# Memory-attention queries multiplied from the un-normed sum, the first layer norm applied to the product

## The chip, the cores and the metric

The kernel runs on one core of one Trainium2 chip. The metric is the device time of one execution in microseconds (us). Four engines do the work here: TensorE (PE, with its weight loads shown apart as PEld), VectorE (DVE), ScalarE (ACT) and SyncE (SP), which issues the weight transfers. GpSimd (POOL) issues a handful of transfers early and late. Each engine runs its own instructions strictly in the order in which they are written, and waits on semaphores that the others count up.

## What is computed

Two transformer blocks on 256 tokens of width 1024, in float32. The stretch that is changed lies in the first block, between the hybrid mixer and the attention over a memory of 256 rows:

```python
x = layer_norm(ALPHA * x + h, ln1_g, ln1_b)        # h: output of the mixer, ... @ w_out
h = memory_cross_attention(x, mem, xa_wq, xa_wkv, xa_wo)
x = layer_norm(ALPHA * x + h, ln2_g, ln2_b)

def layer_norm(x, g, b):
    mu = x.mean(-1, keepdims=True)
    var = square(x - mu).mean(-1, keepdims=True)
    return (x - mu) * rsqrt(var + EPS) * g + b

def memory_cross_attention(x, mem, wq, wkv, wo):
    q = (x @ wq).reshape(B, S, 4, 256)             # four heads
    k, v = split(mem @ wkv)
    p = softmax(einsum('bshd,bmhd->bhsm', q, k) * 256 ** -0.5)
    return einsum('bshm,bmhd->bshd', p, v).reshape(B, S, 1024) @ wo
```

## The kernel before

Activations lie transposed: the width on the partitions in 8 tiles of 128, the 256 tokens along a row. `X` holds the residual stream. Every large product is made in three passes of fp32r: an operand is split into a high half (ACT rounds it) and a low half (DVE subtracts), and PE adds high x high, low weight x high, high weight x low (`three`). For activations these halves lie in `INH`/`INL` or in `HIH`/`HIL`, for weights in `hir`/`lor`.

A **unit** is 256 output columns: 8 tiles of the width, two halves of 128 columns, three passes, 48 matmuls. Its weights come as two chunks of 4 tiles (512 KB, in a ring of 6 raw buffers), and each chunk is split on ACT (`hir`, 128x1024) and then on DVE (`lor`, 128x1024) into one of 4 slots. `Ahead.take` writes these splits into the programs of ACT and DVE: before a unit's own work it splits as far as three chunks ahead, where the slot's earlier matmuls stand earlier in the program. The plan also interleaves chunks for a modulation vector of the second block, which only DVE handles (`raw<-raw,cb`, L1628). `ahead.more()` splits one chunk ahead by itself.

The work around the change, in order:

- Four units `("wout", c)` make the mixer's output. After each, DVE adds it to the residual (`resid`, L1614, `X<-X,ps`) and ACT squares the sum (`SQ`, L1253). PE adds up the row sums by one-column matmuls (`row_sums`): an early part over tiles 0 to 5, then tiles 6 and 7. Before the last unit ACT loads the function table for the square root.
- `layer_norm("n1", ...)`: DVE copies the sums (L1888), makes the variance, ACT takes the root (L1267), DVE the reciprocal (L1896). PE spreads mean and reciprocal over the partitions (`spread_bank`, banks `("n1", "mu")` and `("n1", "r")` of PSUM). DVE subtracts and multiplies in `X`, ACT writes the normed high halves into `INH` (L1272) and the affine result into `X` (L1277), DVE the low halves into `INL`.
- Four units `("xq", c)`, one for each head, the first two interleaved tile by tile, read those halves. DVE copies each product to `QC` (`query`, L1936).
- The attention, head by head: `("lx", i)` are the scores of head i, `("px", h)` the transposes, `("ox", h)` the product with the values. DVE takes the maximum (L1949), ACT the exponential (L1297) and the copies. Then four units `("xo", c)` and the second norm.

PSUM has eight banks: three for units (`lin`), five for all else (`att`). Both pools hand out banks in a ring; a bank taken with `hold` is skipped until it is released, and who takes a bank waits until its previous user's reader has signalled.

The kernel already treats two units of the second block, `("q", 2)` and `("k", 2)`, in the way that the change extends: `late_g` multiplies an un-normed input `xg` with a few extra columns behind the 256 tokens (260 in all) and holds the halves of a unit in one bank of `lin` and one of `att`. DVE settles the product there in pieces (L2137, L1614, L1611), and ACT's part of it (L1407) stands after the splits of the next unit.

## Time and profile before

| | us |
|---|---|
| median of 3 runs | 892.78 |
| lowest, highest | 890.99, 893.64 |
| the profiled execution, its own time | 890.62 |
| its span in the trace | 888.8 |
| PE busy | 851.0 |
| DVE busy | 651.0 |
| ACT busy | 483.1 |
| mean granted TensorE clock | 0.977 of full |

The profiled execution spends 1.8 us outside the span. In the trace the four `wout` units end at 184.96 us, the first `xq` matmul starts at 192.11, the first scores at 218.02, and the first `xo` unit at 236.75. In a timeline each row gives start, time from the first start to the last end of what it merges, engine, line, operation, tiles and shapes, how many, and in brackets how long the engine had been idle and for whom. Consecutive instructions overlap a little, so the distance of two starts is what one costs in a queue.

### The profile page before, as it was taken

Reading aid. Unit: us, or ns where it says so; the run is one execution under the profiler, and the core shown is the slowest. Engines: PE = TensorE matmul, PEld = TensorE weight load, DVE = VectorE, ACT = ScalarE, POOL = GpSimd, SP = SyncE. Lnnn points to the kernel's source line nnn. Section 1 sums busy time; section 2 is a strip of 40 time slices with the busy share of each in tenths; the row PEclk is TensorE's granted clock in tenths of the full one; section 3 lists DMA queues with packets and bytes.
Section 4 is the critical chain, followed back from the end, with each engine's and each line's share of the span. In section 5 each row is a group of like instructions: output and inputs, shape, how many; then the busy total and the mean of one; then the engine's idle time right before and its main releaser. Section 6 shows DMA issues by size and latency. Waiting matters only on the chain.

```text
span 888.8 us, 15825 instructions
## 1 busy us (share of the span) xinstructions
PE 851.0 (96%) x6396; PEld 803.5 (90%) x6396; DVE 651.0 (73%) x1011; ACT 483.1 (54%) x708; POOL 7.6 (1%) x17
## 2 busy tenths in 40 slices
PE   8999998999999999999997999999999899999997
PEld 7889986989889999999996999898998899999885
DVE  5787787777668888888867895787897866655553
ACT  5643456555447666655546745465646654444452
POOL 0200000000000000000000000000000000000000
PEclk9999999979999999999998999999998899999999
DMA  9886658737052765567852554475565276775751
GB/s 336 230 274 210 214 172 257 223 113 255 26 164 92 222 188 186 174 202 254 265 200 71 154 179 132 132 240 184 186 204 159 80 255 214 236 232 180 177 193 48
DMA packets 139592, 166.89 MB, mean 188 GB/s; under 512 B 5520, under 2 KB 123280, under 8 KB 139520
## 3 DMA queue, kind: packets, MB, share of 16 engines
q1 hardware_dynamic: 137712, 162.82, 57.8%
q0 software_dynamic: 720, 2.02, 1.2%
q8 instruction: 50, 0.82, 0.4%
q10 hardware_dynamic: 1088, 1.05, 0.3%
q14 instruction: 22, 0.18, 0.1%
HBM read 164.62 MB, written 1.25 MB: 187 GB/s over the span
## 4 chain that ended last, share of the span: by engine, by line
PE 67%; DVE 19%; ACT 7%; issue 4%; DMA 1%; SPq 1%; DVEq 0%; ACTq 0%
PE ps L520 66%; DVE lor L1611 7%; DVE FA L1611 3%; DVE FA L1614 3%; ACT hir L1104 2%; DMA raw<-in_w_in 1%; DVE FA L1617 1%; DVE raw L1628 1%; DVE X L1611 1%; DVE INL L1611 1%; ACT FA L1297 0%; DVE FA L2297 0%; ACT FA L1230 0%; ACT FA L1490 0%; DVE X L1614 0%
## 5 line engine op out<-in xcount | busy, mean ns | idle before, releaser
L1611 DVE TENSOR_TENSOR lor<-raw,hir 128x1024 fp32r<-128x1024 f32 (+1 forms) x267 | 309.7, 1177 | 110.8 <-ACT hir L1104 107.5
L1104 ACT ACTIVATE hir<-raw 128x1024 fp32r<-128x1024 f32 (+1 forms) x257 | 260.5, 1032 | 125.6 <-PE ps L520 112.6
L520 PE MATMUL ps<-INH,hir 128*128 128x256 f32 (+1 forms) x1064 | 306.5, 288 | 5.1 <-ACT INH L1272 2.5
L520 PE MATMUL ps<-INH,lor 128*128 128x256 f32 (+1 forms) x1064 | 302.7, 285 | 3.3 <-DVE lor L1611 3.3
L520 PE MATMUL ps<-INL,hir 128*128 128x256 f32 (+1 forms) x1064 | 303.2, 285 | 1.5 <-DVE INL L1611 1.3
L520 PEld LDWEIGHTS ps<-INH,hir 128*128 128x128 f32 x1064 | 204.6, 192 | 8.2 <-issue 5.8
L520 PEld LDWEIGHTS ps<-INH,lor 128*128 128x128 f32 x1064 | 204.2, 192 | 5.5 <-DVE lor L1611 4.3
L520 PEld LDWEIGHTS ps<-INL,hir 128*128 128x128 f32 x1064 | 203.9, 192 | 3.0 <-DVE INL L1611 2.8
L520 PE MATMUL ps<-HIH,hir 128*128 128x256 f32 x688 | 196.9, 286 | 0.0
L520 PE MATMUL ps<-HIH,lor 128*128 128x256 f32 x688 | 194.1, 282 | 2.3 <-DVE lor L1611 2.3
L520 PE MATMUL ps<-HIL,hir 128*128 128x256 f32 x688 | 193.2, 281 | 0.0
L520 PEld LDWEIGHTS ps<-HIH,hir 128*128 128x128 f32 x688 | 129.8, 189 | 3.9 <-issue 3.5
L520 PEld LDWEIGHTS ps<-HIH,lor 128*128 128x128 f32 x688 | 129.5, 188 | 3.4 <-DVE lor L1611 2.7
L520 PEld LDWEIGHTS ps<-HIL,hir 128*128 128x128 f32 x688 | 130.0, 189 | 0.0
L1614 DVE SCALAR_TENSOR_TENSOR FA<-ps,vec,FA 128x254 f32<-128x254 f32 (+2 forms) x130 | 53.2, 473 | 14.5 <-ACT FA L1114 14.4
L520 PE MATMUL ps<-hir,HIH 128*128 128x512 f32 (+1 forms) x136 | 52.8, 388 | 6.5 <-DVE HIL L1611 6.5
L1628 DVE SCALAR_TENSOR_TENSOR raw<-raw,cb 128x1024 f32<-128x1024 f32 x48 | 58.3, 1219 | 0.8 <-DMA raw<-in_mod_wT 0.8
L520 PE MATMUL ps<-lor,HIH 128*128 128x512 f32 (+1 forms) x136 | 52.3, 385 | 0.0
L520 PE MATMUL ps<-hir,HIL 128*128 128x512 f32 (+1 forms) x136 | 52.3, 384 | 0.0
L1114 ACT ACTIVATE FA<-ps,vec 128x256 f32<-128x256 f32 x58 | 29.3, 556 | 30.0 <-PE ps L520 30.0
L520 PE MATMUL ps<-FA 128*128 128x256 f32 (+6 forms) x212 | 39.2, 365 | 2.5 <-DVE FA L1611 1.7
L1611 DVE TENSOR_TENSOR HIL<-FA,HIH 128x512 fp32r<-128x512 f32 (+2 forms) x32 | 22.0, 689 | 22.5 <-ACT HIH L1109 21.8
(271 smaller groups left out, 771.0 us busy)
## 6 DMA issues: line engine op xcount, KB each, us to landing
raw<-in_w_in SPq DMA_DIRECT2D x64, 512.0 KB, 4.5
raw<-in_mod_wT SPq DMA_DIRECT2D x48, 512.0 KB, 4.7
raw<-in_ffn_w_up SPq DMA_DIRECT2D x44, 512.0 KB, 4.3
raw<-in_w_ffn_in SPq DMA_DIRECT2D x44, 512.0 KB, 4.6
raw<-in_w_ffn_out SPq DMA_DIRECT2D x22, 512.0 KB, 4.6
raw<-in_ffn_w_down SPq DMA_DIRECT2D x20, 512.0 KB, 4.9
raw<-in_xa_wkv SPq DMA_DIRECT2D x16, 512.0 KB, 4.5
raw<-in_xa_wq SPq DMA_DIRECT2D x8, 512.0 KB, 5.1
```

The costliest lines, as they stand in the source:

```text
L520: return e.matmul(o, l, r, start=start, stop=stop, skip_group_check=True)
L1104: e.activation(hi, src, ACT.Copy).then_inc(*w_hi.up(i))
L1114: e.activation(o[:, b, :], p[:, b * T:(b + 1) * T], ACT.Identity, scale=V(wname, (K - 1) * nb + i + b), bias=V(bname, i + b)).then_inc(*ac ...
L1611: return e.tensor_tensor(o, a, b, op)
L1614: return e.scalar_tensor_tensor(out=o, in0=a, scalar=s, in1=b, op0=op0, op1=op1)
L1617: return e.tensor_scalar(o, a, s1, s2, op0, op1) if op1 else e.tensor_scalar(o, a, s1, None, op0)
L1628: e.scalar_tensor_tensor(out=v, in0=v, scalar=1.0, in1=CB[:, :], op0=MUL, op1=MUL, accum_out=MOD[:, key[1]:key[1] + 1]).then_inc(*dve.up(key))
```

## The change

With G the gains and B the offsets of the first norm, m and r the mean and the reciprocal deviation of a token, and y the un-normed sum, the query is W'(G(y - m)r + B) = (W'Gy - (W'G)m)r + W'B. So:

- `xg1` is a new input in `HIH`/`HIL`: the un-normed sum scaled by `ln1_g` (`gained(c)`, two instructions on ACT and two on DVE for each of the four `wout` units), and two extra columns, `ln1_g` and `ln1_b`, whose products are W'G and W'B.
- The first tile's step of `xq` 0 and 1 stands right behind the last `wout` unit, the second one between the early and the late row sums, the third before the two spreads, the other five after them (`late_g`, 258 columns instead of 256).
- The normed high and low halves in `INH`/`INL` fall away. `X` still gets its norm: DVE's `normed(c)` and eight affine instructions on ACT.
- `query` falls away. In its place stands `settle(c)`: on DVE two copies of two columns, two SCALAR_TENSOR_TENSOR (m(W'G) - product), and one multiplication by r, read from the bank `("n1", "r")`; then on ACT two instructions that negate and add W'B. The scores of head i wait for ACT's `QC` now.
- `xq` units take a bank of `lin` and one of `att` each; the four of `att` are held until all four units have been issued.

```diff
+            g = late_g([("xq", 0), ("xq", 1)], xg1, 2)
+            steps_of(g, 1)
+            row_sums("n1", 3, X[:, 6:8, :], g)
+            steps_of(g, 1)
+            spread_bank(("n1", "mu"), SN[:, 0:2])
+            spread_bank(("n1", "r"), SN[:, 6:8])
+            run(g)
...
+            for c in (2, 3):
+                run(late_g([("xq", c)], xg1, 2))
...
-                    w.wait_ge(copied(before), dve.at(("QC", i)), act.at("KV"))
+                    w.wait_ge(copied(before), act.at(("QC", i)), act.at("KV"))
...
+            def gained(c):
+
+                for k in (2 * c, 2 * c + 1):
+                    w.wait_ge(dve.at(("n1", "x", c)), vec_in.at(0), mm.at("xg1 free"))
+                    e.activation(xg1.hi[:, k, 0:T], X[:, k, :], ACT.Copy, scale=V("ln1_g", k)).then_inc(*act.up(("xg1", "hi", k)))
...
+            def settle(c):
+                for j in range(2):
+                    w.wait_ge(dve.at((("xq", c), "normed")))
+                    e.activation(QC[:, 2 * c + j, :], QC[:, 2 * c + j, :], ACT.Identity, scale=-1.0, bias=GB2[c % 2][j][:, 1:2]).then_inc(
+                        *act.up(("QC", c)))
...
+            for k in range(8):
+                w.wait_ge(dve.at(("n1", "normed", k // 2)))
+                e.activation(X[:, k, :], X[:, k, :], ACT.Identity, scale=V("ln1_g", k), bias=V("ln1_b", k)).then_inc(*act.up(("n1", "affine")))
+            ahead.more()
+            settle(0)
+            ahead.more()
+            settle(1)
+            for c in (2, 3):
+                ahead.unit(("xq", c), 8)
+                settle(c)
...
+            def settle(c):
+
+                key, dst = ("xq", c), QC[:, 2 * c:2 * c + 2, :]
+                for j in range(2):
+                    b, vs = bank["unit", key, j], GB2[c % 2][j]
+                    w.wait_ge(mm.at(("unit", key, j)), *([act.at(("QC", c - 2))] if c >= 2 else []))
+                    e.tensor_copy(vs, b[:, T:T + 2]).then_inc(*dve.up())
+                    w.wait_ge(dve.last(), act.at("mean row"), *before)
+                    stt(dst[:, j, :], MB, vs[:, 0:1], b[:, 0:T], MUL, SUB).then_inc(*dve.up(("out", ("unit", key, j))))
+                w.wait_ge(dve.last(), mm.at(("n1", "r")))
+                tt(dst, dst, over(br[:, 0:T], 2), MUL).then_inc(*dve.up((key, "normed"), ("out", ("n1", "r"))))
```

On ACT, from the root of the norm to the first exponential, this stands before:

```order
L1267 ACTIVATE small<-small 128x2
L1272 ACTIVATE INH<-X,vec 128x256 x4
L1277 ACTIVATE X<-X,vec 128x256 x2
L1272 ACTIVATE INH<-X,vec 128x256 x2
L1277 ACTIVATE X<-X,vec 128x256 x2
L1272 ACTIVATE INH<-X,vec 128x256 x2
L1277 ACTIVATE X<-X,vec 128x256 x2
L1104 ACTIVATE hir<-raw 128x1024 x7
L1297 ACT_TABLE_LOAD
```

and this after, where L1326 is the affine part, L1307 the settling and L1119 the high halves of weight chunks:

```order
L1320 ACTIVATE small<-small 128x2
L1322 ACTIVATE st<-ps 128x256
L1119 ACTIVATE hir<-raw 128x1024 x2
L1326 ACTIVATE X<-X,vec 128x256 x8
L1119 ACTIVATE hir<-raw 128x1024
L1307 ACTIVATE FA<-FA,small 128x256 x2
L1119 ACTIVATE hir<-raw 128x1024
L1307 ACTIVATE FA<-FA,small 128x256 x2
L1119 ACTIVATE hir<-raw 128x1024
L1307 ACTIVATE FA<-FA,small 128x256 x2
L1119 ACTIVATE hir<-raw 128x1024 x2
L1307 ACTIVATE FA<-FA,small 128x256 x2
```

The seven splits, which stood in one piece, stand apart now, with the two instructions of a settled unit between them.

On DVE the same place, from the norm's last product to the third settled unit, reads like this after the change (L1654 `lor` are the low halves of chunks; L2014, L1657 and `FA<-FA,ps` are `settle`):

```order
L1654 TENSOR_TENSOR X<-X,ps 128x512
L1654 TENSOR_TENSOR lor<-raw,hir 128x1024
L2014 COPY small<-ps 128x2
L1657 SCALAR_TENSOR_TENSOR FA<-st,small,ps 128x256
L2014 COPY small<-ps 128x2
L1657 SCALAR_TENSOR_TENSOR FA<-st,small,ps 128x256
L1654 TENSOR_TENSOR FA<-FA,ps 128x512
L1654 TENSOR_TENSOR lor<-raw,hir 128x1024
```

Where two copies of a whole unit stood one behind the other, each unit now has five instructions, with the low half of a chunk ahead of each unit's five.

On PE, with the numbers of the banks, the spreads and the first scores stand like this after the change:

```order
L524 MATMUL ps3<-con,small 128x128 x2
L524 MATMUL ps4<-con,small 128x128 x2
...
L524 MATMUL ps4<-FA 128x256 x4
L524 MATMUL ps5<-FA 128x256 x4
L848 MATMUL ps6<-con,FA 128x128 x4
```

Before, the spreads went to `ps6` and `ps7` and the first scores to `ps3`; now the first scores take `ps4`, the bank of the reciprocal, whose last reader is the fourth `settle` on DVE.

## Rows read from the trace of the kernel before

**Rows 1.** The page's first part: busy time, share, instructions.

```profile
span 888.8 us, 15825 instructions
...
PE 851.0 (96%) x6396; PEld 803.5 (90%) x6396; DVE 651.0 (73%) x1011; ACT 483.1 (54%) x708; POOL 7.6 (1%) x17
```

**Rows 2.** Stretches: length, busy PE, PEld, DVE, ACT, POOL, then PEclk, DMA, GB/s.

```profile
185.00:188.40 3.40, 2.85 (x25) 2.68 (x24) 1.36 (x3) 1.58 (x2) 0.00 (x0) 1.00 0.74 249
188.40:192.00 3.60, 2.25 (x8) 1.86 (x8) 2.29 (x9) 0.80 (x2) 0.00 (x0) 0.50 0.18 60
...
198.00:200.00 2.00, 2.00 (x17) 2.00 (x16) 1.97 (x4) 0.82 (x3) 0.00 (x0) 0.84 0.19 60
...
218.00:220.00 2.00, 2.00 (x12) 1.77 (x11) 0.74 (x2) 0.00 (x0) 0.00 (x0) 1.00 1.00 342
...
222.00:224.00 2.00, 1.19 (x8) 1.12 (x9) 1.48 (x5) 0.41 (x2) 0.00 (x0) 1.00 0.01 3
```

**Rows 3.** Timeline of PE, 184.5 to 226 us.

```profile
184.96 0.28 PE L520 MATMUL ps<-con,st 128*128 128x1 f32 x2
...
186.42 1.05 PE L520 MATMUL ps<-con,X 128*128 128x1 f32 x8 [0.51 <-DVE X L1614]
...
193.34 0.41 PE L520 MATMUL ps<-INH,hir 128*128 128x256 f32 x1
193.55 0.41 PE L520 MATMUL ps<-INH,lor 128*128 128x256 f32 x1
...
218.02 3.62 PE L520 MATMUL ps<-FA 128*128 128x256 f32 x16
222.81 0.66 PE L833 MATMUL ps<-con,FA 128*128 128x128 f32 x4 [1.17 <-DVE FA L1617]
```

**Rows 4.** Timeline of DVE, 165 to 205 us.

```profile
170.52 1.23 DVE L1611 TENSOR_TENSOR lor<-raw,hir 128x1024 fp32r<-128x1024 f32 x1 [1.72 <-ACT hir L1104]
...
183.40 2.36 DVE L1611 TENSOR_TENSOR lor<-raw,hir 128x1024 fp32r<-128x1024 f32 x2 [0.57 <-ACT hir L1104]
185.68 0.68 DVE L1614 SCALAR_TENSOR_TENSOR X<-X,ps 128x512 f32<-128x512 f32 x1
188.40 0.16 DVE L1888 COPY small<-ps 128x4 f32<-128x4 f32 x1 [2.04 <-PE ps L520]
...
189.43 0.17 DVE L1896 RECIPROCAL small<-small 128x2 f32<-128x2 f32 x1 [0.27 <-ACT small L1267]
...
194.92 1.40 DVE L1611 TENSOR_TENSOR X<-X,ps 128x512 f32<-128x512 f32 x2
...
202.70 1.22 DVE L1628 SCALAR_TENSOR_TENSOR raw<-raw,cb 128x1024 f32<-128x1024 f32 x1
```

**Rows 5.** Timeline of ACT, 165 to 198 us.

```profile
180.20 0.63 ACT L1253 ACTIVATE SQ<-X 128x512 f32<-128x512 f32 x1 [2.44 <-DVE X L1614]
...
182.26 1.99 ACT L1104 ACTIVATE hir<-raw 128x1024 fp32r<-128x1024 f32 x2
...
195.38 1.09 ACT L1277 ACTIVATE X<-X,vec 128x256 f32<-128x256 f32 x2
196.38 1.08 ACT L1272 ACTIVATE INH<-X,vec 128x256 fp32r<-128x256 f32 x2
```

**Rows 6.** Timeline of DVE at the settled units of the second block.

```profile
491.55 0.15 DVE L2137 COPY small<-ps 128x3 f32<-128x3 f32 x1
...
492.84 0.69 DVE L1611 TENSOR_TENSOR FA<-FA,st 128x512 f32<-128x512 f32 x1
493.45 0.15 DVE L2137 COPY small<-ps 128x3 f32<-128x3 f32 x1
```

**Rows 7.** Timelines of PE and ACT at the 260-column units.

```profile
461.58 0.29 PE L520 MATMUL ps<-INH,hir 128*128 128x260 f32 x1
461.70 0.28 PE L520 MATMUL ps<-INH,lor 128*128 128x260 f32 x1
...
462.28 0.89 ACT L1365 ACTIVATE INH<-X,small 128x256 fp32r<-128x256 f32 x2
```

## What I predict, and from which rows

> **What bounds the kernel now.** I read the page's busy times first: PE is busy for 851.0 of 888.8 us, DVE for 651.0, ACT for 483.1 [rows 1]. So in most of the program PE sets the pace, and the question is what happens in the one place where it does not. The table by stretches shows that place. Around the first norm PE has only one-column matmuls, the spreads and waits: 2.85 us busy of 3.40 and 2.25 of 3.60, and in the second of these stretches the granted clock is 0.50 (1.2 of 2.4 GHz), after PE had done nothing but one-column matmuls and waited since 184.96. It stays there while the first query matmuls run and is back only within 198 to 200 (mean 0.84 there) [rows 2, 3]. PE's timeline gives the prices: query matmuls start 0.21 us apart at the low clock [rows 3], and the 260-column ones elsewhere 0.12 apart at the full one [rows 7]. The last `wout` matmul is followed at 184.96 by the first row sum, and the first scores start at 218.02 [rows 3]. These 33.1 us hold 192 query matmuls, which at 0.12 are 22.9 us. That is the most that the change could work on: about 10 us, of which some 2.9 are the low clock (30 matmuls at 0.095 more each) and the rest the norm.
>
> Then I read DVE and ACT, because the change gives PE a start without the norm, but gives DVE and ACT more to do, and puts the two in a row.
>
> **The change, part by part.**
>
> *Ahead of the query units.* `gained` adds two ACT instructions per `wout` unit; the nearest row, a scaled copy of 256 columns, is 0.89 for two, about 0.8 in a queue [rows 7]. DVE gets two 256-column instructions, again about 0.8. Before the second unit's splits DVE was idle for 1.72 us for ACT's high half [rows 4]: ACT's extra work (0.8 and 0.3 for the extra columns) lengthens this very wait. So the sums come later by about 1.0 to 1.2 us at unit 2; bounds are 0 (all in idle time) and 1.9 (both units in full). I take 1.2. At unit 3 ACT's chain is square at 180.20, table, high halves at 182.26 [rows 5], low halves at 183.40, residual sum at 185.68 [rows 4]; 0.8 for `gained` goes in between. The last residual sum moves from 185.68 to 185.68 + 1.2 + 0.8 = 187.7.
>
> *PE up to the sums.* The first chunk of `xq` 1 is the first of the two low halves that started at 183.40; it is done at 183.4 + 2.0 + 1.15 = 186.5. PE starts at 184.96 with 6 products, waits until 186.6, does 6 more (187.3), the early sums (0.9: 188.2), the second tile's 12 products (1.4: 189.65) and the late sums, which took 188.40 - 186.42 = 1.98 from their start to DVE's copy [rows 3, 4]: 191.6. DVE's five small instructions take 189.43 - 188.40 = 1.03 to the reciprocal [rows 4]: it is past at 192.75. PE hides its part of this behind products, which is what the change does well; PE is not late for anything from here on.
>
> *DVE's queue behind the reciprocal.* In the order after the change stand three low halves (1.14 each, from 2.36 for two [rows 4]), two modulation chunks (1.14 in a queue [rows 4]) and four pairs that norm `X` (1.40 for two dependent ones, 1.32 in a queue [rows 4]): 3.42 + 2.28 + 5.28 = 10.98, so the last pair is done at 203.75. Before, PE read the normed halves; now nobody does, but this work still stands ahead of the first `settle`.
>
> *ACT in the same place.* Its affine instructions wait for these pairs. The last two (1.09 for two, 1.0 in a queue [rows 5]) end at 204.8, then the high half of the next chunk (0.96 in a queue, 1.05 alone, from 1.99 for two [rows 5]) at 205.85, DVE's low half (0.1 of waiting and 1.14) at 207.1. There `settle(0)` starts. Its inputs have lain in PSUM since about 201.
>
> *The round trip.* This is the term that decides. `settle` on DVE is 1.90 from its first copy to the next instruction, and its last instruction is done 0.08 later: 1.98 [rows 6]. ACT's `settle` waits for that (0.03) and takes 1.0 [rows 5]. The next high half stands behind it on ACT (1.05), the next low half waits for that (0.1 and 1.14), and the next DVE `settle` stands behind the low half. Neither engine has other work in between, apart from one modulation chunk of 1.14 that fits into DVE's wait. One round is 1.98 + 0.03 + 1.0 + 1.05 + 0.1 + 1.14 = 5.3. So the units settle from 207.1, 212.4, 217.7 and, with a second low half in the last round, 217.7 + 5.3 + 1.14 = 224.1. A product unit needs 48 x 0.12 = 5.8, so PE keeps up: it ends its last unit 24 products after the chunk split at 212.4, at about 215.3.
>
> *Who waits for it.* The first scores take the bank that holds r, and so wait for the fourth `settle`: 224.1 + 1.98 + 0.05 = 226.15. Against 218.02 that is **+8.1**. Even with another bank DVE's maximum of the first scores would stand behind the fourth `settle`, so the bank alone costs only some 2. ACT's last two `settle` instructions and its table load run beside the scores. Before, the copy of a unit ran beside PE and this place cost nothing; cover is gone because both engines wait for each other. Bounds: 6 if `gained` hides in idle time and the rounds are 5.0, 9.5 if the sums come 1.9 later and a split waits for its slot on top.
>
> *The clock at the scores.* PE is empty from 215.3 to 226.15. No row shows PE empty for so long here; the nearest are the stretches around the norm, where far less brought 0.50 [rows 2]. So the attention starts at the low clock. Its first two heads' scores take 3.62 at full clock, and the first transposes start 4.8 after the first score [rows 3]; at half they take 7.2, and the transposes follow them: +2.4. If the clock is back half way through, it is +1.7. At the norm it was back some 6 us after the query matmuls began in earnest, so I take **+2.2**; the bounds are 0 (no fall) and the third rival. The later scores and transposes hide behind DVE and ACT as now: PE is busy for 1.19 of 2.00 there [rows 2].
>
> Here the Trainium skill says something else ("TensorE: Matmul & The Clock Gate", "Part 4: PE-mode transpose"): transposes do not count as activity for the clock gate. In both stretches of the attention that stand here, the second of them with transposes, the clock is 1.00 [rows 2], but it came in at full clock. By the rule the attention could stay low for longer after such a start; with the row the term is 2.2, with the rule up to 14.
>
> *At no cost:* the two extra columns (192 x 0.001 = 0.2 us of PE, which has 10.8 to spare); the transfers, which now wait for later splits but have raw buffers loaded ahead; the second norm's wait for `X`, which is done at 204.8.
>
> Sum: 890.62 + 8.1 + 2.2 = 900.9 against the profiled execution's own time. The median of the runs shown lies 2.2 above that execution, which gives 903.1. I take the middle, **902.0**.
>
> **Rivals.**
>
> 1. *PE sets the end (faster).* If the waits between ACT and DVE were shorter than PE's work, the stage would end with PE: 184.96 + 0.9 (first wait) + 22.9 + 2.9 (sums) + 0.8 (spreads) = 212.5, and the scores after the last `settle` at 214.5: -3.5, or 889.3 on the median. It decides from the point where a round costs less than about 2.8, which needs ACT's splits to run ahead of its `settle`; the order of the program speaks against it. For it speaks that PE stays dense and may keep its clock. The Trainium skill's rule points this way ("TensorE: Matmul & The Clock Gate", "Loop structure matters more than you think"): matmuls that stand back to back stay warm, and vector work behind them does not break it. Chance 0.04.
> 2. *The round trip is hidden.* If only DVE's own work counted, 1.14 + 1.90 a unit: last `settle` from 207.1 + 3 x 3.04 + 1.14 = 217.4, scores at 219.4, +1.4, with part of the clock's loss 894 to 896. Chance 0.05, of which 0.02 within the noise.
> 3. *The whole attention at the low clock.* 64 records of the scores' kind at 0.226 and 16 transposes at 0.12 are 16.4 us; at half 32.8 against the 18.7 that the attention takes: +14. With 8.1 that is 915. Against it: at half clock PE would be busy without a pause, and at the norm such a stretch brought the clock back. Chance 0.04.
>
> **How the numbers follow.** The forecast has 0.87. Its own range runs from +6 with a small loss of clock to +9.5 with 3.4: 897.5 to 907. That leaves out the rivals and little else, so it is the range for 8 in 10. A measurement can tell 0.3% (2.7 us) from no change. Faster by more: 0.04. Within: 0.03. Slower by more: 0.93.
>
> **What would show it.** Right: in the profile after, `lor` on DVE waits for ACT's `hir`, and `FA<-FA,small` on ACT for DVE, about 2 to 3 us each, four times; the four settled units start 5.3 apart; the first scores start near 226 and wait for DVE `FA`; PE is empty for about 10 us before; the granted clock there is 0.50. Wrong: rounds under 4 us, or first scores before 220; or PE late for a split, with the idle time spread over its 192 matmuls. The first unknown is the size of the wait at the sums, the second the clock.

## The result, and the profile after

| | before | after |
|---|---|---|
| median of the runs, us | 892.88 | 902.70 |
| lowest to highest | 890.99 to 893.64 | 898.90 to 904.97 |
| ratio, with its 95% interval | | 1.0112 [1.0088, 1.0136] |
| own time of the profiled execution | 890.62 | 902.05 |
| its span | 888.8 | 900.2 |
| mean granted TensorE clock | 0.977 | 0.972 |

The kernel became slower, by 9.8 us. A second measurement of the same two kernels gave 1.0120 [1.0098, 1.0142]. The page's first part barely moved against [rows 1]: each engine has a few microseconds more work, and the span is 11.4 longer, so the time is a wait.

```profile
span 900.2 us, 15860 instructions
...
PE 852.9 (95%) x6396; PEld 804.9 (89%) x6396; DVE 655.2 (73%) x1028; ACT 487.0 (54%) x721; POOL 7.6 (1%) x17
```

One thing has to be set aside before the traces are compared. The first residual sum of the `wout` units starts at 168.12 in before and at 170.86 in after, though the code ahead of it is the same. In thirteen traces of kernels that are all alike up to there it starts anywhere from 167.69 to 171.25. So I take this instruction as the zero of the place, and write distances from it as "+": the first scores of before, at 218.02, stand at +49.90. The end of the place is DVE's copy of the second norm's sums, at +94.95 in before and +104.20 in after: the changed stretch is **9.25 us longer**. Behind it both kernels take the same time to the end of the span within 0.6 us (625.73 and 625.14); over the thirteen traces this rest is 624.25 to 626.97, so whole times can differ by over 2 us with nothing changed in the place.

The end mark has a weakness of its own. Between the fourth residual sum of the `xo` units and the copy lie sixteen one-column matmuls, and the clock falls in them or behind them, at no fixed place. In after, where it stays at 1.00 until 275.5, the copy comes 2.72 behind that residual sum; in e3_fill, the same code there, the clock is at 0.50 from 272.5 and it comes 3.76 behind. The second eight of the sixteen, in after and in e3_fill:

```profile
273.99 1.03 PE L524 MATMUL ps<-con,SQ 128*128 128x1 f32 x8
...
272.77 1.84 PE L524 MATMUL ps<-con,SQ 128*128 128x1 f32 x8
```

So I also give the fourth `xo` residual sum, at +92.23 in before and +101.48 in after: 9.25 by this mark too. Where the two marks differ between runs, the residual sum is free of that part of the clock.

DVE's timeline answers to [rows 4] (start, time, instruction, shapes, count, idle time before and for whom; L1657 `X<-X,ps` are residual sums, L1989 the copy of the norm's sums, L2014 the first instruction of a `settle`, L2035 the first maximum):

```profile
170.86 0.69 DVE L1657 SCALAR_TENSOR_TENSOR X<-X,ps 128x512 f32<-128x512 f32 x1 [0.36 <-PE ps L524]
...
190.33 0.68 DVE L1657 SCALAR_TENSOR_TENSOR X<-X,ps 128x512 f32<-128x512 f32 x1
...
194.37 0.16 DVE L1989 COPY small<-ps 128x4 f32<-128x4 f32 x1 [1.38 <-PE ps L524]
...
205.94 0.69 DVE L1654 TENSOR_TENSOR X<-X,ps 128x512 f32<-128x512 f32 x1
...
208.83 1.23 DVE L1654 TENSOR_TENSOR lor<-raw,hir 128x1024 fp32r<-128x1024 f32 x1 [2.21 <-ACT hir L1119]
209.97 0.15 DVE L2014 COPY small<-ps 128x2 f32<-128x2 f32 x1
...
215.12 0.15 DVE L2014 COPY small<-ps 128x2 f32<-128x2 f32 x1
...
220.26 0.15 DVE L2014 COPY small<-ps 128x2 f32<-128x2 f32 x1
...
224.22 2.36 DVE L1654 TENSOR_TENSOR lor<-raw,hir 128x1024 fp32r<-128x1024 f32 x2 [1.99 <-ACT hir L1119]
226.50 0.15 DVE L2014 COPY small<-ps 128x2 f32<-128x2 f32 x1
...
231.96 0.69 DVE L2035 TENSOR_REDUCE small<-ps 128x2 f32<-128x512 f32 x1 [3.48 <-PE ps L524]
```

The four `settle`s start 5.15, 5.14 and 6.24 apart. ACT's timeline shows the other half of the same wait: each time ACT stands 3.3 us for DVE's product, settles, and only then begins the high half for which DVE waits:

```profile
211.99 0.91 ACT L1307 ACTIVATE FA<-FA,small 128x256 f32<-128x256 f32 x2 [3.29 <-DVE FA L1654]
212.80 1.04 ACT L1119 ACTIVATE hir<-raw 128x1024 fp32r<-128x1024 f32 x1
217.13 0.91 ACT L1307 ACTIVATE FA<-FA,small 128x256 f32<-128x256 f32 x2 [3.28 <-DVE FA L1654]
```

The waits of 155 to 250 us, summed by who waits for whom (us in total, times, longest). The first group was not there before:

```profile
ACT FA L1307 <- DVE FA L1654: 13.3, 4, 3.4
...
PE ps L524 <- DVE FA L1654: 10.1, 1, 10.1
DVE lor L1654 <- ACT hir L1119: 8.9, 7, 2.4
```

The third was 6.7 in 7 before. No wait for a weight transfer is among them; before there were two, of 2.0 and 0.9.

PE's timeline, answering to [rows 3]: the first scores, and the first transposes behind them.

```profile
228.53 5.11 PE L524 MATMUL ps<-FA 128*128 128x256 f32 x16 [10.06 <-DVE FA L1654]
234.81 0.66 PE L848 MATMUL ps<-con,FA 128*128 128x128 f32 x4 [1.16 <-DVE FA L1660]
```

The table by stretches answers to [rows 2] (columns as there). At the norm and in the products the clock stays at 1.00, where before it was 0.50; it falls in PE's empty time and is back within 230 to 232:

```profile
188.40:192.00 3.60, 2.79 (x24) 2.66 (x23) 2.61 (x3) 1.46 (x4) 0.00 (x0) 1.00 0.36 107
192.00:200.00 8.00, 8.00 (x71) 8.00 (x70) 6.04 (x13) 4.41 (x8) 0.00 (x0) 1.00 0.53 160
...
220.00:224.00 4.00, 0.00 (x0) 0.00 (x0) 2.13 (x6) 1.73 (x3) 0.00 (x0) 0.64 0.66 221
224.00:228.00 4.00, 0.00 (x0) 0.00 (x0) 3.67 (x7) 1.07 (x2) 0.00 (x0) 0.50 0.35 115
228.00:230.00 2.00, 1.47 (x4) 1.20 (x5) 0.48 (x1) 1.47 (x3) 0.00 (x0) 0.50 0.81 241
230.00:232.00 2.00, 2.00 (x8) 1.65 (x7) 0.04 (x1) 0.72 (x1) 0.00 (x0) 0.65 0.15 54
```

So what the change is good at, it did: PE ends its query products at +47.6, where before they ended with the first scores at +49.9. Then it stands empty for 10.06 us, because the two engines behind it wait for each other.

### The profile page after: what moved, and what is told of

Same layout as the page of the kernel before. It is cut to its first block, busy times and chain, and to the rows that moved or that the text cites. A ratio compares the mean times of both kernels' runs of the same rounds, so it can differ in the third digit from the quotient of the medians.

```text
span 900.2 us, 15860 instructions
## 1 busy us (share of the span) xinstructions
PE 852.9 (95%) x6396; PEld 804.9 (89%) x6396; DVE 655.2 (73%) x1028; ACT 487.0 (54%) x721; POOL 7.6 (1%) x17
## 4 chain that ended last, share of the span: by engine, by line
PE 65%; DVE 20%; ACT 8%; issue 4%; DMA 1%; SPq 1%; DVEq 0%; ACTq 0%
PE ps L524 65%; DVE lor L1654 7%; DVE FA L1657 3%; DVE FA L1654 3%; ACT hir L1119 2%; DMA raw<-in_w_in 1%; DVE raw L1671 1%; DVE FA L1660 1%; DVE X L1654 1%; ACT FA L1340 0%; DVE FA L2383 0%; PE ps L766 0%; ACT FA L1245 0%; ACT FA L1533 0%; ACT L1134 0%
## 5 line engine op out<-in xcount | busy, mean ns | idle before, releaser
L1654 DVE TENSOR_TENSOR lor<-raw,hir 128x1024 fp32r<-128x1024 f32 (+1 forms) x267 | 309.7, 1177 | 117.5 <-ACT hir L1119 112.6
L1119 ACT ACTIVATE hir<-raw 128x1024 fp32r<-128x1024 f32 (+1 forms) x257 | 260.2, 1031 | 118.8 <-PE ps L524 110.6
L524 PE MATMUL ps<-INH,hir 128*128 128x256 f32 (+1 forms) x1000 | 287.1, 287 | 2.9 <-ACT INH L1602 1.2
L524 PE MATMUL ps<-INH,lor 128*128 128x256 f32 (+1 forms) x1000 | 283.6, 284 | 2.9 <-DVE lor L1654 2.8
L524 PE MATMUL ps<-INL,hir 128*128 128x256 f32 (+1 forms) x1000 | 284.2, 284 | 1.0 <-DVE INL L1654 0.9
L524 PE MATMUL ps<-HIH,hir 128*128 128x256 f32 (+1 forms) x752 | 216.1, 287 | 3.2 <-DVE lor L1654 1.4
L524 PE MATMUL ps<-HIH,lor 128*128 128x256 f32 (+1 forms) x752 | 212.8, 283 | 2.3 <-DVE lor L1654 2.3
L524 PE MATMUL ps<-HIL,hir 128*128 128x256 f32 (+1 forms) x752 | 211.9, 282 | 0.0
L524 PEld LDWEIGHTS ps<-INH,hir 128*128 128x128 f32 x1000 | 191.5, 191 | 5.7 <-issue 4.3
L524 PEld LDWEIGHTS ps<-INH,lor 128*128 128x128 f32 x1000 | 191.0, 191 | 5.1 <-DVE lor L1654 3.9
L524 PEld LDWEIGHTS ps<-INL,hir 128*128 128x128 f32 x1000 | 190.8, 191 | 2.1 <-DVE INL L1654 2.1
L1657 DVE SCALAR_TENSOR_TENSOR FA<-ps,vec,FA 128x254 f32<-128x254 f32 (+2 forms) x130 | 53.2, 473 | 15.1 <-ACT FA L1129 15.1
L524 PEld LDWEIGHTS ps<-FA 128*128 128x128 f32 (+2 forms) x212 | 29.5, 179 | 20.0 <-DVE FA L1654 12.1
```

Of the source, the lines that this page charges most:

```text
L524: return e.matmul(o, l, r, start=start, stop=stop, skip_group_check=True)
L1119: e.activation(hi, src, ACT.Copy).then_inc(*w_hi.up(i))
L1654: return e.tensor_tensor(o, a, b, op)
L1657: return e.scalar_tensor_tensor(out=o, in0=a, scalar=s, in1=b, op0=op0, op1=op1)
```

## The experiments

Theory: the round trip between ACT and DVE in the settled units sets the time, with a small loss from the clock behind it. Rivals: DVE's own work (the normed `X` ahead of the units), the bank of r, and the clock. This table gathers the runs. The stretch is measured as above. The kernel before was timed beside each group (medians 891.46 for e1 to e4, 891.93 for e5 to e8, 890.90 for e9 to e11), so medians of different groups are compared by their ratios. e10_after is the changed kernel once more.

| kernel | median, us | ratio to before [95%] | first scores | first transposes | fourth `xo` sum | stretch | against before |
|---|---|---|---|---|---|---|---|
| before | 892.88 | 1 | +49.90 | +54.69 | +92.23 | 94.95 | |
| after | 902.70 | 1.0112 [1.0088, 1.0136] | +57.67 | +63.95 | +101.48 | 104.20 | +9.25 |
| e1_order | 897.58 | 1.0074 [1.0055, 1.0093] | +52.53 | +59.20 | +96.75 | 100.25 | +5.30 |
| e2_twice | 904.03 | 1.0153 [1.0123, 1.0183] | +60.38 | +67.06 | +104.61 | 107.33 | +12.38 |
| e3_fill | 901.80 | 1.0125 [1.0106, 1.0144] | +57.71 | +62.59 | +100.12 | 103.88 | +8.93 |
| e4_later | 891.08 | 0.9996 [0.9984, 1.0007] | +44.57 | +52.42 | +92.26 | 94.98 | +0.03 |
| e5_bank | 902.01 | 1.0122 [1.0106, 1.0138] | +47.52 | +61.85 | +100.76 | 104.22 | +9.27 |
| e6_norms | 897.26 | 1.0065 [1.0052, 1.0079] | +44.56 | +57.56 | +96.90 | 100.48 | +5.53 |
| e7_best | 886.80 | 0.9950 [0.9938, 0.9963] | +44.56 | +49.34 | +88.72 | 93.06 | -1.89 |
| e8_warm | 891.90 | 1.0006 [0.9990, 1.0022] | +49.73 | +54.51 | +92.05 | 94.77 | -0.18 |
| e9_best | 887.85 | 0.9959 [0.9944, 0.9973] | +44.58 | +49.37 | +87.52 | 90.23 | -4.72 |
| e10_after | 902.94 | 1.0120 [1.0098, 1.0142] | +57.71 | +64.22 | +101.76 | 104.48 | +9.53 |
| e11_fill | 900.56 | 1.0101 [1.0081, 1.0120] | +57.71 | +62.60 | +100.16 | 102.91 | +7.96 |

### The round trip

**e1_order** takes the round trip apart by ACT's order alone; each instruction is still there.

```diff
             ahead.more()
-            settle(0)
             ahead.more()
-            settle(1)
+            settle(0)
             for c in (2, 3):
                 ahead.unit(("xq", c), 8)
-                settle(c)
+                settle(c - 1)
+            settle(3)
```

> The changed kernel with one thing altered: on ScalarE the high halves of the next chunks stand ahead of settle(0), settle(1), settle(2) and settle(3) instead of between them; VectorE's and TensorE's programs are untouched. Theory (round trip): in the changed kernel's trace the settled units start 5.15, 5.14 and 6.24 us apart, because VectorE's low half waits for a high half that waits for ScalarE's settle. Without it the distances fall to VectorE's own work: 3.0 (1.14 + 1.90), 4.2 (a modulation chunk more) and 4.2 (two low halves), in all 11.4 instead of 16.5, so the first scores start 5 us earlier than in the changed kernel and the kernel takes about 897.5. Rival (TensorE or the transfers set the stage): the distances stay, 902.7. Second rival (only the clock costs): distances fall, but the time stays within 1 us of 902.7.

Measured 897.58. That is 5.1 below the changed kernel, but the two were not timed side by side; by the ratios 3.4 of the 10.0 us are back. In the trace of e1_order DVE's settled units follow each other after 3.03, 4.17 and 4.17 us, which is DVE's own work (one low half and one `settle`, in two cases a second half or a modulation chunk):

```profile
206.91 0.15 DVE L2014 COPY small<-ps 128x2 f32<-128x2 f32 x1
...
209.94 0.15 DVE L2014 COPY small<-ps 128x2 f32<-128x2 f32 x1
...
214.11 0.15 DVE L2014 COPY small<-ps 128x2 f32<-128x2 f32 x1
...
218.28 0.15 DVE L2014 COPY small<-ps 128x2 f32<-128x2 f32 x1
```

Its fourth `settle` stands at +50.50 instead of +55.64, the first scores come 5.14 earlier, and the fourth `xo` residual sum 4.73 of the 9.25. Only ACT's order was changed, so about half of the loss is the round trip.

**e2_twice** lengthens it: two more instructions of 256 columns on ACT in each `settle`, that copy `QC` onto itself.

```diff
+                for j in range(2):
+                    w.wait_ge(act.last())
+                    e.activation(QC[:, 2 * c + j, :], QC[:, 2 * c + j, :], ACT.Copy).then_inc(*act.up(("QC", c)))
```

> The changed kernel with two more 256-column instructions on ScalarE behind each settle (a copy of QC onto itself), nothing else. Two such instructions take 0.8 us in a queue, and the second pair waits for the first (some 0.1). Theory (round trip): each of the three rounds grows by 0.9, the first scores start 2.7 us later against the changed kernel (the fourth pair runs beside the scores, and the table load behind it still ends before the first maximum), 905.5 in all. Rival (ScalarE has idle time there, 3.3 us before each settle, so more work on it is hidden): no change, 902.7.

In the trace of e2_twice a round costs 6.04, 6.04 and 7.13 us:

```profile
207.36 0.15 DVE L2017 COPY small<-ps 128x2 f32<-128x2 f32 x1
...
213.40 0.15 DVE L2017 COPY small<-ps 128x2 f32<-128x2 f32 x1
...
219.44 0.15 DVE L2017 COPY small<-ps 128x2 f32<-128x2 f32 x1
...
226.57 0.15 DVE L2017 COPY small<-ps 128x2 f32<-128x2 f32 x1
```

That is 0.9 a round more, on an engine that is busy for half of the time, and the scores come 2.71 later, as expected. If ACT had slack there, it would have cost nothing. Both traces speak for the round trip; the stretch moved by 3.13 here, the median by only 1.3 (904.03, where I expected 905.5), with intervals that overlap, so the times alone do not show it.

### The bank and the normed residual

**e5_bank** frees the bank of r: ACT copies the spread row to SBUF, DVE reads it there.

```diff
+            w.wait_ge(mm.at(("n1", "r")))
+            e.activation(RB, bank["n1", "r"][:, 0:T], ACT.Copy).then_inc(*act.up("r row", ("out", ("n1", "r"))))
...
-                w.wait_ge(dve.last(), mm.at(("n1", "r")))
-                tt(dst, dst, over(br[:, 0:T], 2), MUL).then_inc(*dve.up((key, "normed"), ("out", ("n1", "r"))))
+                w.wait_ge(dve.last(), act.at("r row"))
+                tt(dst, dst, over(RB, 2), MUL).then_inc(*dve.up((key, "normed")))
```

> The changed kernel with one edit: ACT copies the spread reciprocal from its PSUM bank to SBUF, DVE reads it there, and the bank is free for the first scores. This is the step of my prediction that gave the bank alone only some 2 us: with it free the scores run while the last units are settled, but DVE's first maximum still stands behind the fourth settle on DVE, and ACT's table load behind the fourth settle on ACT. From the trace after: the fourth settle ends on DVE at 228.4, ACT's part at 229.4, table load 1.28, first exponentials 1.0, so the first transposes at about 232.7 instead of 234.81: 2.1 us less, part of it given back since the transposes now are the first work after PE's idle time. Theory (round trip sets the time, bank adds about 2): 900.5 to 901.5 where the changed kernel is 902.7. Rival (the wait for the bank, not the round trip, is what the change lost): the whole 8 us come back, 894.

Neither PE's wait nor its size was the loss. The scores run at +47.52, ten microseconds earlier, and the kernel is no faster (902.01, where I expected 900.5 to 901.5). The first transposes did come 2.1 earlier, as expected (+61.85), but now they are the first work after PE's empty time. The stretches of e5_bank show PE empty, the clock fallen, and back only in 231 to 233:

```profile
224.00:229.00 5.00, 0.00 (x0) 0.00 (x0) 2.36 (x8) 3.21 (x7) 0.00 (x0) 0.50 0.59 191
229.00:231.00 2.00, 1.40 (x6) 1.31 (x7) 1.32 (x4) 0.61 (x3) 0.00 (x0) 0.50 0.00 0
231.00:233.00 2.00, 2.00 (x7) 1.61 (x6) 0.78 (x3) 0.89 (x3) 0.00 (x0) 0.58 0.00 0
```

In after, the first scores run while the clock comes back; here the transposes and the second scores do. From the first transposes to the first `xo` residual sum it is 21.37 instead of 19.99. So of the 2.10 some 0.72 are left at the fourth `xo` residual sum, and these are gone in the one-column matmuls behind it, where the clock had fallen (+9.27).

**e6_norms** is e5_bank with the norm of `X`'s tiles 2 to 7 moved from ahead of the first `settle` into the attention.

```diff
             run(late)
-            for c in (1, 2, 3):
-                normed(c)
             ahead.more()
...
                     ts(nmx, mxx, -0.0625, None, MUL).then_inc(*dve.up(("nmx", i)))
+                    if i:
+                        normed(i)
```

> e5_bank and one edit more: the norm of X's tiles 2 to 7 (three pairs on DVE, six affine instructions on ACT) is moved from ahead of the first settle to inside the attention, behind the first maxima and copies. It tells what the normed residual costs where it stands, by itself, with the round trips left as they are. From the trace after: three pairs are 3.96 us in DVE's queue and six affine instructions 3.0 on ACT ahead of the split that settle(0) waits for. Theory: the first settle comes about 4.0 earlier, the rounds stay at 5.15, 5.15 and 6.2, and the attention pays about 1 for the pairs (1.32 each in waits of 1.09): 3 us under e5_bank, about 898. Rival (DVE's own queue is not the bound there, ACT's wait for slots that PE frees is): settle(0) moves by less than 2, and the time by nothing.

The first `settle` stands at 203.82, which is +34.87 instead of +39.11: 4.2 earlier. The rounds stay 5.14, 5.15 and 6.25. The stretch is 3.74 shorter than in e5_bank (3.86 at the fourth `xo` residual sum), the median 4.7 lower, timed side by side. So the work that nobody waits for any more (PE reads other halves now) was the second part of the loss, about 4 us, by standing where it stood.

**e4_later** has all three edits: e1_order's order on ACT, e5_bank's row, e6_norms's place for the norm. Parts of its edit on ACT:

```diff
             ahead.more()
-            settle(0)
             ahead.more()
-            settle(1)
+            settle(0)
             for c in (2, 3):
                 ahead.unit(("xq", c), 8)
-                settle(c)
+                settle(c - 1)
+            settle(3)
...
                     e.activation(PY[:, h % 2, :, :], wide2(bank["px", h]), ACT.Copy).then_inc(*act.up(("out", ("px", h))))
+                    affine(h)
```

> As e1_order, and three things more: ScalarE copies the reciprocal's row to SBUF, so that the bank of the spread is free at once; VectorE's norm of X for tiles 2 to 7 (3.96 us) stands in the attention, behind the maximum of heads 1 to 3, instead of ahead of settle(0); ScalarE's affine part follows it there. Theory (VectorE's queue ahead of the first settle is on the path): the first settle starts 3.8 us earlier than in e1_order, and the first scores about 9 us earlier than in the changed kernel; the norms add at most 0.3 us per head to the attention. 892.5 to 894.5. Rival (TensorE ends the stage, or the norms are paid back in the attention one for one): the same as e1_order, about 897.5.

It is as fast as the kernel before, 891.08 (0.9996 [0.9984, 1.0007]), 1.4 below the range that I expected. At the fourth `xo` residual sum the three parts add up: 4.73 for ACT's order, 0.72 for the bank and 3.86 for the norm make 9.31, and e4_later is 9.22 below after. (By the stretch the two large parts are only 3.95 and 3.74, since in e1_order and e6_norms, and not in e4_later, the clock fell within the one-column matmuls.) What was left shows in the timelines of e4_later, PE's first:

```profile
213.84 3.62 PE L524 MATMUL ps<-FA 128*128 128x256 f32 x16
221.69 1.12 PE L848 MATMUL ps<-con,FA 128*128 128x128 f32 x4 [4.23 <-DVE FA L1666]
```

ACT's, with the fourth settled unit and the load of the function table:

```profile
217.55 0.91 ACT L1307 ACTIVATE FA<-FA,small 128x256 f32<-128x256 f32 x2 [3.26 <-DVE FA L1660]
218.47 1.28 ACT L1345 ACT_TABLE_LOAD   x1
```

DVE's, with two low halves and the start of the fourth `settle`:

```profile
213.26 2.35 DVE L1660 TENSOR_TENSOR lor<-raw,hir 128x1024 fp32r<-128x1024 f32 x2
215.53 0.15 DVE L2020 COPY small<-ps 128x2 f32<-128x2 f32 x1
```

PE is done with the products 5.3 us before the kernel before was, and then waits 4.23 us: two low halves of the next unit stand ahead of the fourth `settle`, and the table of the exponential stands behind it.

### The clock

**e3_fill** keeps PE at work with 70 products into an unused bank, between the last unit and the scores.

```diff
+            j = lin.i % 3
+            w.wait_ge(*[dve.at(("out", ("unit", ("xq", 1), x))) for x in range(2)])
+            for _ in range(70):
+                mul(lin.aps[j][:, 0:256], xg1.hi[:, 0, 0:128], xg1.hi[:, 1, 0:256])
```

> The changed kernel with 70 fp32r matmuls of 256 columns behind the last query unit on TensorE, into a bank that the next unit overwrites; they need 8.3 us of the 10.3 for which TensorE is empty, so the first scores can't come later by them. Theory of the clock term: with TensorE kept busy the granted clock stays at its upper level (1.00 instead of 0.50 to 0.65 in the stretches at 228 to 232), the first two heads' scores take 3.6 instead of 4.7 to 5, and the attention's first maximum comes 1.6 us after the first scores instead of 3.4: 1.6 to 2.4 us off, about 900.8. Rival: the clock has nothing to do with the empty stretch, no change.

The trace of e3_fill, PE's timeline: scores of 3.72 for 16 instead of 5.11, transposes 4.88 behind them instead of 6.28.

```profile
228.48 3.72 PE L524 MATMUL ps<-FA 128*128 128x256 f32 x16 [1.78 <-DVE FA L1658]
233.36 0.66 PE L852 MATMUL ps<-con,FA 128*128 128x128 f32 x4 [1.16 <-DVE FA L1664]
```

The time did not settle it: 1.0125 against 1.0112, where I expected 0.2% less. Both kernels were then timed side by side:

> The changed kernel once more, unedited, on the same chip as e11_fill, since the two had been timed at different occasions, where the kernel before differed by 1.4 us. By the ratio of the first measurement (1.0112) it is 1.1% above the kernel before beside it, 901.5 if that is 891.5. It also shows whether the stage from the first wout residual to the last xo residual is 101.5 again.

> e3_fill once more, unedited, beside e10_after: the changed kernel with 70 product matmuls into an unused bank ahead of the first scores, so that PE comes to them at the full clock. In the traces the stage was 1.36 us shorter than in the changed kernel (100.12 instead of 101.48); the times, taken at two occasions, did not show it. Theory (the low clock costs the change about 1.4): 1.0 to 1.8 us below e10_after. Rival (it costs nothing, what comes late at the scores is waited for elsewhere anyway): equal to e10_after within 0.5.

902.94 and 900.56, 2.4 apart, but the intervals of the ratios overlap ([1.0098, 1.0142] and [1.0081, 1.0120]). The traces agree: the first transposes come 1.36 and 1.62 earlier with the filler, and so does the fourth `xo` residual sum (1.36 and 1.60). I take the clock's price as about 1.5 us; the times are compatible with it and alone don't show it.

The traces also tell why it is no more. The transposes wait for a chain of DVE and ACT that starts with DVE's first maximum, and the maximum needs only the first head's eight scores, not all sixteen. The first maximum in before, and the first maximum and the first transposes in e1_order:

```profile
219.95 0.69 DVE L1949 TENSOR_REDUCE small<-ps 128x2 f32<-128x512 f32 x1 [1.04 <-PE ps L520]
...
224.12 0.69 DVE L2035 TENSOR_REDUCE small<-ps 128x2 f32<-128x512 f32 x1 [3.88 <-PE ps L524]
...
226.98 0.66 PE L848 MATMUL ps<-con,FA 128*128 128x128 f32 x4 [0.52 <-DVE FA L1660]
```

The maximum comes 1.93 behind the first scores in before, 3.43 in after, 3.66 in e10_after, 3.81 in e1_order and 3.83 in e2_twice. The transposes follow it by 2.85 or 2.86 in all five and in both runs with the filler, and the first `xo` residual sum follows them by 20.0 in all seven. In e1_order the clock came back only some 5 us after the scores began, and the lag was still 1.9 above before's.

**e8_warm** looks at the clock on the other side: it puts products between the small matmuls at the norm of the kernel before (`fill(n)` is n products of 256 columns).

```diff
-            layer_norm("n1")
+            row_sums("n1", 3, X[:, 6:8, :])
...
+            fill(3)
+            spread_bank(("n1", "mu"), SN[:, 0:2])
+            fill(4)
+            spread_bank(("n1", "r"), SN[:, 6:8])
+            fill(7)
```

> The kernel before with 14 product matmuls of 256 columns into an unused bank: 3 behind the row sums, 4 behind the spread of the mean, 7 behind the spread of the reciprocal. Nothing else is changed, and their result is not used. It takes the price of the clock out of the 10 us that the change could work on. Theory (some 2.9 us of them are the 30 query matmuls at 0.21 instead of 0.12): the granted clock stays 1.00 from 188.4 on, query matmuls start 0.12 apart, and the kernel is 2 to 2.9 us faster than the kernel before, 888.6 to 889.5 where that is 891.5. Rival (the first query units wait for ACT and DVE anyway, so that the clock costs nothing): no difference; PE then waits for halves between its query matmuls.

No difference (891.90, 1.0006 [0.9990, 1.0022]). But the edit did not do all that it was meant to: the clock still fell, to 0.50 in 190 to 192. It came back earlier, in the stretch 192 to 194 instead of 198 to 200. Then PE waits for what the low clock had hidden, as its timeline shows (the first row is the first query matmul):

```profile
193.87 0.36 PE L520 MATMUL ps<-INH,hir 128*128 128x256 f32 x1
...
194.71 0.39 PE L520 MATMUL ps<-INL,hir 128*128 128x256 f32 x1 [0.37 <-DVE INL L1623]
...
196.81 0.39 PE L520 MATMUL ps<-INL,hir 128*128 128x256 f32 x1 [0.42 <-DVE INL L1623]
...
199.08 0.39 PE L520 MATMUL ps<-INL,hir 128*128 128x256 f32 x1 [0.58 <-DVE INL L1623]
```

With the clock up, the first products are paced by DVE's normed low halves, 2.1 and 2.3 us apart; with the clock down, in before, a tile's twelve products at 0.21 take 2.6 and PE does not wait. The fillers themselves made the first query matmul 0.61 later (+24.60 instead of +23.99), and from it to the first scores it is 25.13 instead of 25.91. So the clock there was worth 0.8 of the 2.9 us that I had put down to it, as far as this run shows it, and the fillers took that back. What a clock that never falls would give stays open.

### A version that is faster than both

**e7_best** is e4_later with what its trace asked for. Parts of the edit, against e4_later; `preload` stands on ACT, all else on DVE:

```diff
             for c in (2, 3):
+                ahead.limit = AHEAD if c == 2 else 0
                 ahead.unit(("xq", c), 8)
                 settle(c)
...
+            preload(ACT.Exp)
             settle(3)
...
-                    if i:
-                        normed(i)
+                    if i < 2 and ahead.room():
+                        ahead.stage()
...
+                    if h < 2:
+                        normed(h + 1)
...
+                if c == 0:
+                    normed(3)
```

> From the version with the splits ahead of the settling and the norms of X later (891.1, its trace: fourth settle at 215.53, reduce 217.43, first transposes 221.69 at the low clock, 7.9 us behind the first scores). Edits: on DVE the two low halves of the first output unit are moved from ahead of the fourth settle into the first two waits for the exponentials; ACT loads the table of the exponential ahead of its fourth settle; the pairs of X's norm go into waits of 0.77 and behind the first output unit's splits. Theory: the fourth settle starts as soon as PE is done, at about 214.1, the reduce follows at 216.0, the transposes at about 218.9, 5.1 us behind the scores as in the kernel before, so PE is idle for 1.4 us only and keeps its clock; the first residual sum of the output units comes 4.5 to 5 us earlier: 886 to 887, faster than both kernels. Rival (something else, such as the transfers of weights or DVE's low halves in the attention, sets the time once this is gone): over 889.

886.80, ratio 0.9950 [0.9938, 0.9963]: faster than the kernel before by 0.5%. The fourth `settle` starts 0.34 after PE, and the attention begins as dense as before the change, at the full clock, 5.35 us earlier than there (+49.34 against +54.69). DVE's timeline of e7_best:

```profile
212.09 0.16 DVE L2026 COPY small<-ps 128x2 f32<-128x2 f32 x1 [0.34 <-PE ps L525]
...
214.18 0.69 DVE L2047 TENSOR_REDUCE small<-ps 128x2 f32<-128x512 f32 x1
```

PE's timeline of e7_best:

```profile
212.25 3.62 PE L525 MATMUL ps<-FA 128*128 128x256 f32 x16
217.03 0.66 PE L849 MATMUL ps<-con,FA 128*128 128x128 f32 x4 [1.16 <-DVE FA L1672]
```

**e9_best** cuts the moved norms in two and puts each half into a gap of its own on DVE.

```diff
                     if i < 2 and ahead.room():
                         ahead.stage()
+                    if i >= 2:
+                        (norm_sub, norm_mul)[i - 2](1)
...
-                    if h < 2:
-                        normed(h + 1)
+                    (norm_sub, norm_mul)[h % 2](2 + h // 2)
...
-                if c == 0:
-                    normed(3)
```

> e7_best with the norm of X put into shorter gaps. In e7_best the first residual sum of the output units waited 1.24 us for ACT's last affine instructions (it started at 240.68, the second at 245.36, 4.7 behind instead of 5.7), and the pairs of 1.32 stood in waits of 0.77. Edits: each norm is cut into its subtraction and its multiplication, 0.61 each, one for each wait of DVE in the attention (two for the exponentials of heads 2 and 3, four behind the copies of the product with the values), and the affine instructions follow in the same heads, the last ahead of the splits. Theory: the residual sum no longer waits, the attention loses the 0.5 per head that the pairs cost, and the stage from the first wout residual to the last xo residual shrinks from 88.7 to about 87: 885 to 886. Rival (PE in the output units is bound by other things, and the late sum cost nothing): within 0.5 us of e7_best, 886.8.

The residual sum no longer waits. The fourth `xo` residual sum comes 1.20 earlier than in e7_best. The stretch shrank by 2.83, to 90.23, but the other 1.63 lie in the one-column matmuls behind that sum, where the clock was at 0.50 in e7_best and at 1.00 in e9_best. The median is 887.85, where I expected 885 to 886: level with e7_best, since the intervals [0.9944, 0.9973] and [0.9938, 0.9963] overlap. A gain of 1.2 is less than these times can show.

## Why the prediction came out right

The forecast was 902.0 with 897.5 to 907.0; the measured median is 902.7. Step by step, each as the distance from the first residual sum (168.12 in before, from whose times the forecast counts, 170.86 in after):

| step of the prediction | forecast | measured |
|---|---|---|
| last residual sum (187.7) | +19.58 | +19.47 |
| sums reach DVE (191.6) | +23.48 | +23.51 |
| last pair of the norm done (203.75) | +35.63 | +35.77 |
| first `settle` (207.1) | +38.98 | +39.11 |
| second, third (212.4, 217.7) | +44.28, +49.58 | +44.26, +49.40 |
| fourth `settle` (224.1) | +55.98 | +55.64 |
| first scores (226.15) | +58.03 | +57.67 |
| first transposes (222.81 + 8.1 + 2.2) | +64.99 | +63.95 |

- *Ahead of the units.* The size was right (1.9 for 2.0), and so was the wait: the low half at 170.52 for which DVE was idle for 1.72 [rows 4] starts at +3.40 instead of +2.40, and the next residual sum, the second unit's, stands at +6.83 instead of +5.83.
- *DVE's queue and the round trip.* Right, 5.15 for 5.3. The price of a `settle` on ACT was 0.81 in its queue, not 1.0: I had taken it from affine instructions with two vectors [rows 5], while `settle` has a constant scale. e1_order and e2_twice show that this term decides, and e6_norms shows that the queue ahead of it was the other half of the loss.
- *The bank.* Given as "only some 2": 2.1 at the first transposes, 0.7 at the fourth `xo` residual sum and nothing in the time (e5_bank), since the low clock moves onto the transposes.
- *The clock.* The term that was mis-sized. Forecast 2.2; the transposes lag by 1.5 (6.28 behind the scores instead of 4.79), by 1.7 in e10_after, and the fillers give the same. Two things were off. I let the transposes follow all sixteen scores, which gave 2.4 at the low clock; they follow the first eight, by way of DVE's maximum, and with all eight at the low clock the lag is 1.9 (e1_order, e2_twice). And I allowed for a clock that comes back only some 6 us after work begins, by the norm's example; in after it came back in under 3, so that not even the eight were all slow.
- *What the change could work on.* I put 2.9 of some 10 us down to the clock at the norm; in e8_warm 0.8 of them came back, and the fillers took them again. This changed no term of the sum.
- *The total.* The stretch grew by 9.25 against 10.3 in the sum; the medians differ by 9.8 against 9.1, since I had taken the middle of 900.9 and 903.1. The agreement to 0.7 us is partly luck: the spread of the lead alone is 3.6 us.

On the rivals: *PE sets the end* needed "ACT's splits to run ahead of its `settle`". That was not enough: e1_order does it, with rounds of 3.03 and 4.17 us, and PE still stands empty for 6.56 us, because the norm of `X` holds up the first `settle`. Only with the norm moved and the bank freed too (e4_later) does PE set the time of the first scores, and only e7_best keeps the attention dense behind it and lands at 886.8, where I had written 889.3. The changed program stands on the other side. There the Trainium skill's rule ("TensorE: Matmul & The Clock Gate", "Loop structure matters more than you think") agrees with the trace: through the products of after the granted clock is 1.00 from 184 to 220, with waits of PE of 0.8 to 1.5 between them. *The round trip is hidden* is excluded by the distances of 5.15 in after and of 6.04 in e2_twice. *The whole attention at the low clock* did not come: in after the clock is back by 232, and in e5_bank, where transposes are the first work after the empty time, within 231 to 233. By the Trainium skill ("TensorE: Matmul & The Clock Gate", "Part 4: PE-mode transpose"), by which a transpose "doesn't count as PE-busy the same way", this could have lasted longer. The traces do not bear it out: with transposes first it lasted 3 us in e5_bank and over 5 in e4_later, and with scores first it lasted from under 3 in after to some 5 in e1_order.

## What to carry to other kernels

When a change puts a step on one engine behind a step of another, read both orders for work that the first engine needs from the second and that stands behind the new wait: here the high half of the next chunk, 1.04 us, behind a `settle` that waits 3.3 us. Work whose reader the change takes away must also move, or it stays in the queue at full price. And a bank that seems to cost something at the place of a wait is worth little until the wait behind it is gone: here 10 us at the first scores, 0.7 at the fourth `xo` residual sum. Each repair alone moved that sum by 0.7 to 4.7 us, all together (e7_best) by 12.8.

## What the hardware showed that I had not expected

- Identical code takes from 167.69 to 171.25 us to the same instruction in thirteen traces, while the distance to the next mark, the fourth residual sum, is 19.46 to 19.48 in eleven of them and 17.56 in the two with the old code. Differences of a stretch are known far better than those of whole runs.
- The clock comes back after an empty time at no fixed distance. Read in pieces of half a microsecond, it is back 2.5 to 3.0 us after the scores begin in after, 3.0 to 3.5 in e10_after, the same kernel, and 4.7 to 5.2 in e1_order. With transposes first it is 2.9 to 3.4 in e5_bank, 3.0 to 3.5 in e6_norms and 5.3 to 5.8 in e4_later. What stands first does not tell the short ones from the long ones, and no run here shows what does.
- The clock falls at no fixed instruction either. In before it is at 0.50 from 188.4, after one-column matmuls and waits [rows 2]; in after, with twelve products between the early and the late sums and twelve behind these, it stays at 1.00. That the products do it is likely, not shown: at the second norm, where neither kernel has them, the sixteen one-column matmuls ran at 1.00 to their end in after, and mostly at 0.50 in e7_best and e6_norms.
